# Expert gate marks built as packed 16-bit products with the tokens innermost, and the index products of all heads in one instruction

## The chip, the cores and the metric

The kernel runs on one core of one Trainium2 chip. The metric is the device time of one execution in microseconds (us); the kernel before and the changed kernel are compared by the median of their runs.

## The reference, cut to what matters

The network has four mixer layers, a neighbourhood-attention block and, at the end, a product-key expert layer (`peer_ffn`). The change lies in that last layer alone, for 512 tokens, 8 heads and 128 x 128 experts:

```python
q = (xb @ wq).reshape(PEER_BLOCK, PEER_HEADS, 2, PEER_HALF)
s = jnp.einsum('thpd,hpkd->thpk', q, sub_keys)
s_top, i_top = lax.top_k(s, PEER_TOPK)                      # 16 of 128, per half
cand_s = (s_top[:, :, 0, :, None] + s_top[:, :, 1, None, :])
best_s, best_pos = lax.top_k(cand_s.reshape(...), PEER_TOPK)
experts = jnp.take_along_axis(cand_i, best_pos, axis=-1)
g = jax.nn.softmax(best_s, axis=-1)
act = jax.nn.gelu(einsum('thkd,td->thk', expert_u[experts], xb))
out = einsum('thk,thkd->td', g * act, expert_v[experts])
```

The kernel gathers no expert. It computes the hidden value of every expert for every token and multiplies it by a gate matrix that is zero but for the 128 chosen pairs of a token (8 heads x 16). `expert = first * 128 + second`, so the gate of one token is a 128 x 128 matrix: a product of one-hot rows of `second` (marks B) with one-hot rows of `first` times the gate (marks A).

## The kernel before, in words

Five engines run their own programs: TensorE (PE), VectorE (DVE), ScalarE (ACT), GpSimd (POOL), and SyncE (SP), which issues the weight loads. They meet through semaphores; each engine's order is the order in which its code is written.

**Expert layer, first half (`hidden_units`).** 32 slots of 512 experts pass through two ring buffers. In each slot four chunks `j` are split in two parts (ACT at L1586 makes the first, POOL at L2502 the second; `second_parts`), PE does 16 matmuls of 512 columns for each chunk (L1144, L1145), ACT applies gelu (L1625). Slots 14 to 29 also make the gates: after each chunk's 16 matmuls PE does 16 small ones of 128 columns (`gate_groups`, L1165), B marks stationary, A marks moving, once for the high part of the gate (`l` = 0) and once for its rest (`l` = 1); ACT moves the result to SBUF (L1616) with tokens innermost, and it is stored to DRAM.

**Routing (DVE, `routing`).** While PE runs the first slots, DVE picks the top 16 for four token tiles `t`. L2265 adds candidate scores, one instruction for each head. For each half `s`, L2288 compares positions with a ruler (128 x 2048), L2291 multiplies by the key indices, one instruction of 128 x 256 for each head, and L2295 sums. `r_shifted` (at L2281 of the last tile) lets ACT take the softmax exponent, and ACT does nothing else until then. L2300 is the last step of the choice.

**Turning the choice.** PE finishes slot 12, stops in `turn_choices` until the choice is made (L1139, 12 transposes), then does slot 13. ACT copies the three turned matrices from PSUM (L1649) for DVE.

**Marks (DVE, `gate_marks`).** 32 batches of 16 tokens (`GC`), two buffers. For each token L2316 is one instruction (compare the 128 numbers with `first`, times the two gate parts, 256 results); L2323 makes the B marks of the batch (128 x 2048, 16-bit). PE waits at chunks 0 and 2 of each slot for a batch; DVE waits before batch n until PE has used batch n - 2.

Of the kernel before, what the change touches and what calls it, by code (L numbers as in the profile page):

```python
# [5 lines left out]
P = 128  # L6
D = 1024
S = 512
# [17 lines left out]
PEER_HEADS, N_KEYS = 8, 128  # L26
# [98 lines left out]
def build(nc, wstream, cols_d, const_d, rows_d, pos_d, x_d, ctx_d, rpb_d, ws_d, out_d):  # L125
# [9 lines left out]
    ds = bass.ds  # L135

    with ExitStack() as ctx:
# [310 lines left out]
        R_SUM = area(1856, 16)  # L448
        R_BV = area(6144, NT, 8, 16)
        R_E = area(6656, NT, 3, P)  # L450
        E_T = [trig.rearrange("p a t c -> p (a t c)"), rs[:, 0, :], rs[:, 1, :]]

        U_SLOTS = N_KEYS // 4
        GATE_FROM, GATE_TO = 14, 30
# [6 lines left out]
        G_B = area(28672, 2, GC, N_KEYS // 2).bitcast(f16)  # L461
        G_IOTA = area(30720, N_KEYS // 2).bitcast(f16)
        G_PARTS = area(30784, 2, S)
        G_ROUND = area(31808, S // 2).bitcast(f16)
        G_SECOND = area(32064, S // 2).bitcast(f16)
        GATE_SCALE = 32768.0
        SPREAD = 128.0
        E_CHUNKS = ROWS_S * U_SLOTS
# [106 lines left out]
        def _(pe):  # L575
# [571 lines left out]
            def hidden_units():  # L1147

                made, used, taken = signal("e_parts_made"), signal("e_parts_used"), signal("u_taken")
                first_hot, second_hot = signal("g_a_made"), signal("g_b_made")  # L1150
                gated, kept = signal("g_summed"), signal("g_kept")

                def gate_groups(i, p, j):

                    batch = 2 * (2 * i + p - GATE_FROM) + j // 2
                    if j % 2 == 0:
                        pe.wait_ge(first_hot, batch + 1)
                        pe.wait_ge(second_hot, batch + 1)
                    for x in range(2):
                        g, b = 8 * (2 * i + p - GATE_FROM) + 2 * j + x, 2 * (j % 2) + x  # L1160
                        if not (isinstance(g, int) and g < 4):
                            pe.wait_ge(kept, g - 3)
                        for t in range(4):
                            for l in range(2):
                                mm = pe.matmul(bank[:, 4 + b, t * P:(t + 1) * P], G_B[:, j // 2, 4 * b + t, :],  # L1165
                                               G_A[:, j // 2, 4 * b + t, l, :], start=(l == 0), stop=(l == 1))
                        mm.then_inc(gated, 1)

                def slot(i, p, gates=False):
                    for j in range(4):  # L1170
                        pe.wait_ge(made, 8 * i + 4 * p + j + 1)
                        if not (first(i) and p == 0):
                            pe.wait_ge(taken, 8 * i + 4 * p + j - 3)
                        for k in range(KT):
                            mm = expert_product(bank[:, j, :], j, k, h2_rounded[:, k, :], h2_rest[:, k, :],
                                                k == 0, k == KT - 1)
                        mm.then_inc(used, 1)
                        if gates:
                            gate_groups(i, p, j)

                def both(i, gates=False):
                    slot(i, 0, gates)
# [102 lines left out]
        def _(act):  # L1285
# [318 lines left out]
            def hidden_units():  # L1604
# [134 lines left out]
        def _(dve):  # L1739
# [506 lines left out]
            def routing():  # L2246
# [4 lines left out]
                for t in range(NT):  # L2251
# [7 lines left out]
                    if t == 0:  # L2259
# [1 line left out]
                    sv = R_SV.rearrange("p (h s) j -> p h s j", s=2)  # L2261
                    ins = v.tensor_tensor(R_CAND[:, :, 0:16], sv[:, :, 0, 0:1].broadcast_to([P, 8, 16]),
                                          sv[:, :, 1, :], ALU.add)
                    for h in range(PEER_HEADS):
                        ins = v.tensor_tensor(  # L2265
                            R_CAND[:, h, 16:136].rearrange("p (i j) -> p i j", i=15),
                            sv[:, h, 0, 1:16].rearrange("p (i a) -> p i a", a=1).broadcast_to([P, 15, 8]),
                            sv[:, h, 1, 0:8].rearrange("p (a j) -> p a j", a=1).broadcast_to([P, 15, 8]), ALU.add)
# [17 lines left out]
                    for s in range(2):  # L2286

                        order(v.tensor_tensor(R_EQ, R_RF[:, s, :].rearrange("p (k a) -> p k a", a=1)  # L2288
                                              .broadcast_to([P, P, 16]), iota16, ALU.is_equal))
                        for h in range(PEER_HEADS):  # L2290
                            ins = v.tensor_tensor(R_EQ2[:, h * 16:(h + 1) * 16, :], R_EQ[:, h * 16:(h + 1) * 16, :],  # L2291
                                                  sif[:, h, s, :].rearrange("p (a j) -> p a j", a=1)
                                                  .broadcast_to([P, 16, 16]), ALU.mult)
                        order(ins)
# [12 lines left out]
            def gate_marks():  # L2307
                first_hot, second_hot, gated = signal("g_a_made"), signal("g_b_made"), signal("g_summed")

                def body(m):  # L2310
                    for b in range(2):
                        n = 2 * m + b
                        if not first(m):
                            dve.wait_ge(gated, 4 * n - 4)
                        for t in range(GC):
                            ins = v.scalar_tensor_tensor(  # L2316
                                out=G_A[:, b, t], in0=cst("iota").rearrange("p (l r) -> p l r", l=1)
                                .broadcast_to([P, 2, N_KEYS]), scalar=E_T[0][:, ds(n * GC + t, 1)],
                                in1=G_PARTS[:, :, ds(n * GC + t, 1)].broadcast_to([P, 2, N_KEYS]),
                                op0=ALU.is_equal, op1=ALU.mult)  # L2320
                        ins.then_inc(first_hot, 1)
                        e = G_SECOND[:, ds(n * GC, GC)].rearrange("p (t a) -> p t a", a=1)
                        v.tensor_tensor(G_B[:, b], G_IOTA.rearrange("p (a r) -> p a r", a=1)  # L2323
                                        .broadcast_to([P, GC, N_KEYS]), e.broadcast_to([P, GC, N_KEYS]),
                                        ALU.is_equal).then_inc(second_hot, 1)
                dve.wait_ge(signal("choice_moved"), 3)
                v.tensor_copy(G_IOTA, cst("iota"))
                v.tensor_copy(G_SECOND, E_T[1])
                order(v.tensor_scalar(G_ROUND, E_T[2], GATE_SCALE, None, ALU.mult))
                order(v.tensor_copy(G_PARTS[:, 0, :], G_ROUND))  # L2330
                order(v.scalar_tensor_tensor(out=G_PARTS[:, 1, :], in0=E_T[2], scalar=GATE_SCALE,
                                             in1=G_PARTS[:, 0, :], op0=ALU.mult, op1=ALU.subtract))
                body(0)
                with dve.Fori(1, S // GC // 2) as m:
                    body(m)
# [346 lines left out]
```

## Time and profile before

| | us |
|---|---|
| median of 3 runs (2893.05 to 2898.33) | 2895.91 |
| the profiled execution, its time | 2900.16 |
| its span from first to last instruction | 2898.3 |
| PE busy / DVE busy / POOL busy | 2657.9 / 1856.9 / 1643.7 |
| mean granted TensorE clock, share of full | 0.961 |

The profiled execution is 4.25 us, 0.15%, above the median. Busy shares are means over many stages with different limits; what the change is worth is read from the stretch between 1690 and 2380 us of the span.

### The profile page before, as it was taken

What the parts mean: (1) busy time and instruction counts of PE and PEld (TensorE: products, weight loads), DVE (VectorE), ACT (ScalarE), POOL (GpSimd) and SP (SyncE); (2) the same over time, 40 slices, a digit from 0 to 9 for tenths busy, and PEclk for the clock granted to TensorE, in tenths of its full rate; (3) what the DMA queues carried; (4) which work ended last, traced back from release to release, by engine and by line L of the source; (5) the groups of instructions that cost most, each with busy time, mean ns of one, the idle gap of its engine ahead of it and who ended that gap; (6) DMA issues with size and microseconds to landing.
All of it is one profiled execution on the core that took longest, in us unless ns stands there. A gap on an engine that the chain in (4) does not pass through costs nothing.

```text
span 2898.3 us, 36976 instructions
## 1 busy us (share of the span) xinstructions
PE 2657.9 (92%) x13468; PEld 2140.2 (74%) x13468; DVE 1856.9 (64%) x3298; ACT 949.5 (33%) x1656; POOL 1643.7 (57%) x964
## 2 busy tenths in 40 slices
PE   7999999999899999999899999918777889999998
PEld 6888787678767788788677888816565667888886
DVE  6432398744664444200365079999999966888886
ACT  2001312833474101111242144314343444444443
POOL 4665457965403566646645557616455556666673
PEclk9999999999999999999999999959898999999998
DMA  4223122122342322322213245514454558888883
GB/s 157 87 87 121 58 88 94 31 66 77 110 146 109 116 92 112 109 88 101 98 41 111 92 175 217 217 44 182 170 217 200 217 217 306 290 289 289 289 289 131
DMA packets 139988, 429.93 MB, mean 148 GB/s; under 512 B 8800, under 2 KB 79584, under 8 KB 116704
## 3 DMA queue, kind: packets, MB, share of 16 engines
q1 hardware_dynamic: 125376, 353.40, 33.8%
q10 hardware_dynamic: 7200, 68.68, 6.1%
q0 software_dynamic: 7296, 6.31, 0.9%
q8 instruction: 72, 1.18, 0.2%
q14 instruction: 44, 0.36, 0.0%
HBM read 358.10 MB, written 73.40 MB: 149 GB/s over the span
## 4 chain that ended last, share of the span: by engine, by line
PE 64%; DVE 18%; issue 8%; POOL 6%; DMA 2%; ACT 1%; DVEq 1%; SPq 0%; ACTq 0%; POOLq 0%
PE bank L1144 8%; PE bank L1145 8%; DVE work L2316 6%; PE bank L697 4%; PE bank L698 4%; PE bank L700 4%; POOL rpb_tiles L2464 3%; PE bank L958 3%; PE bank L953 3%; PE bank L954 3%; PE bank L755 3%; PE bank L727 3%; PE bank L749 3%; PE bank L728 3%; PE bank L732 3%
## 5 line engine op out<-in xcount | busy, mean ns | idle before, releaser
L2502 POOL TENSOR_TENSOR expert_parts<-ring,expert_parts 128x1024 fp32r<-128x1024 f32 x256 | 696.3, 2722 | 495.4 <-ACT expert_parts L1586 492.7
L2526 POOL CAST w_parts<-ring 128x1024 fp32r<-128x1024 f32 (+3 forms) x212 | 228.8, 1079 | 636.3 <-DMA ring<-in_wstream 153.0
L2528 POOL TENSOR_TENSOR w_parts<-ring,w_parts 128x1024 fp32r<-128x1024 f32 (+3 forms) x212 | 512.1, 2416 | 17.0
L1586 ACT ACTIVATE expert_parts<-ring 128x1024 fp32r<-128x1024 f32 x256 | 271.2, 1060 | 538.5 <-PE bank L1145 531.0
L1144 PE MATMUL bank<-h_rounded,expert_parts 128*128 128x512 f32 x1024 | 414.0, 404 | 0.7 <-ACT work L1598 0.7
L1144 PE MATMUL bank<-weighted,expert_parts 128*128 128x512 f32 x1024 | 401.9, 393 | 9.9 <-DVE weighted L2348 9.9
L1145 PE MATMUL bank<-h_rest,expert_parts 128*128 128x512 f32 x1024 | 406.1, 397 | 0.0
L1145 PE MATMUL bank<-weighted,expert_parts 128*128 128x512 f32 x1024 | 401.5, 392 | 0.0
L2316 DVE SCALAR_TENSOR_TENSOR work<-const,trig,work 128x256 f16<-128x256 f32 x512 | 346.3, 748 | 0.0
L2348 DVE SCALAR_TENSOR_TENSOR weighted<-weighted,hF 128x512 fp32r<-128x512 f32 x128 | 309.5, 2419 | 51.3 <-ACT weighted L1666 48.1
L1144 PEld LDWEIGHTS bank<-weighted,expert_parts 128*128 128x128 f32 x1024 | 194.2, 190 | 51.2 <-issue 6.0
L1144 PEld LDWEIGHTS bank<-h_rounded,expert_parts 128*128 128x128 f32 x1024 | 197.9, 193 | 41.5 <-ACT work L1598 0.9
L1145 PEld LDWEIGHTS bank<-h_rest,expert_parts 128*128 128x128 f32 x1024 | 197.5, 193 | 40.1
L1145 PEld LDWEIGHTS bank<-weighted,expert_parts 128*128 128x128 f32 x1024 | 194.3, 190 | 40.7
L697 PE MATMUL bank<-h_parts,w_parts 128*128 128x512 f32 x480 | 186.9, 389 | 0.5 <-POOL w_parts L2528 0.5
L698 PE MATMUL bank<-h_parts,w_parts 128*128 128x512 f32 x480 | 186.8, 389 | 0.0
L1165 PE MATMUL bank<-work 128*128 128x128 f16 x1024 | 74.8, 231 | 89.4 <-DVE work L2323 80.6
L1165 PEld LDWEIGHTS bank<-work 128*128 128x128 f16 x1024 | 63.2, 104 | 109.7 <-issue 109.7
L2353 DVE TENSOR_TENSOR hF<-hF,work 128x512 f32<-128x512 f32 x128 | 97.8, 783 | 46.6 <-DMA work<-gates 46.6
L1518 ACT ACTIVATE work<-bank 128x512 f32<-128x512 f32 (+1 forms) x58 | 32.6, 586 | 264.4 <-PE bank L958 180.7
L700 PE MATMUL bank<-h_parts,w_parts 128*128 128x512 f32 x480 | 118.5, 389 | 0.0
L749 PE MATMUL bank<-w_parts,b_rounded 128*128 128x512 f32 (+3 forms) x320 | 116.9, 372 | 0.7 <-ACT work L1421 0.7
(430 smaller groups left out, 5155.4 us busy)
## 6 DMA issues: line engine op xcount, KB each, us to landing
ring<-in_wstream SPq DMA_DIRECT2D x128, 2048.0 KB, 7.8
hidden<-hF ACTq DMA_DIRECT2D x32, 1024.0 KB, 4.0
gates<-work ACTq DMA_DIRECT2D x16, 2048.0 KB, 10.7
hF<-hidden SPq DMA_DIRECT2D x32, 1024.0 KB, 9.5
work<-gates SPq DMA_DIRECT2D x32, 1024.0 KB, 12.8
rpb_tiles<-in_rpb POOLq DMA_DIRECT2D x192, 16.0 KB, 2.2
work<-rpb_tiles POOLq DMA_DIRECT2D x24, 128.0 KB, 5.4
ring<-in_wstream SPq DMA_DIRECT2D x5, 512.0 KB, 4.0
```

The lines of the kernel that those rows point to most:

```text
L697: pe.matmul(out, w[0][:, k, :], h_parts[:, 0, k, :], start=(k == 0), stop=False)
L698: pe.matmul(out, w[1][:, k, :], h_parts[:, 0, k, :], start=False, stop=False)
L700: mm = pe.matmul(out, w[0][:, k, :], h_parts[:, 1, k, :], start=False, stop=(k == KT - 1))
L749: pe.matmul(out, x, w[0][:, k - ks[0], :], start=(k == 0), stop=False)
L1144: pe.matmul(out, expert_chunk(j, 0)[:, k, :], x, start=start, stop=False)
L1145: return pe.matmul(out, expert_chunk(j, 1)[:, k, :], x_spread, start=False, stop=stop)
L1586: act.activation(expert_chunk(j, 0), ring_chunk(p, j), ACT.Copy, scale=1.0 - 1.0 / SPREAD)\
L2316: ins = v.scalar_tensor_tensor(out=G_A[:, b, t], in0=cst("iota").rearrange("p (l r) -> p l r", l=1) .broadcast_to([P, 2, N_KEYS]), scalar= ...
L2348: v.scalar_tensor_tensor(out=W[:, 4 * p + j, 1, :], in0=W[:, 4 * p + j, 0, :], scalar=1.0 - SPREAD, in1=hF[:, 4 * p + j, :], op0=ALU.mult, ...
L2502: nc.gpsimd.tensor_tensor(expert_chunk(j, 1), ring_chunk(p, j), expert_chunk(j, 0), ALU.subtract).then_inc(made, 1)
L2526: g.tensor_copy(parts[0], source).then_inc(hi, 1)
L2528: g.tensor_tensor(parts[1], source, parts[0], ALU.subtract).then_inc(made, 1)
```

## The change

Four edits. (1) A marks: instead of 16 instructions with 32-bit inputs, a batch takes three 16-bit products of 128 x 2048 with the 16 tokens innermost: a comparison of a ruler with `first`, that times the high part, that times the rest. The moving operand of the small matmuls so becomes one 16-bit number in every 16 (a step of 32 bytes). (2) B marks are made by the same instruction as before, now between the comparison and the products. (3) ACT's three copies go; DVE reads the turned choice from PSUM itself, and writes the ruler before it. (4) In `routing` the eight instructions of L2265 and the eight of L2291 become one each.

```diff
-        G_A = area(24576, 2, GC, N_KEYS).bitcast(f16).rearrange("p b t (l r) -> p b t l r", l=2)
+        G_A = area(24576, 2, 2 * N_KEYS * GC // 2).bitcast(f16).rearrange("p b (l r t) -> p b l r t", l=2, t=GC)
+        G_RULER = area(30720, N_KEYS * GC // 2).bitcast(f16).rearrange("p (r t) -> p r t", t=GC)
+        G_HIGH, G_LOW = (area(31744 + j * S // 2, S // 2).bitcast(f16) for j in range(2))
...
                                 mm = pe.matmul(bank[:, 4 + b, t * P:(t + 1) * P], G_B[:, j // 2, 4 * b + t, :],
-                                               G_A[:, j // 2, 4 * b + t, l, :], start=(l == 0), stop=(l == 1))
+                                               G_A[:, j // 2, l, :, 4 * b + t], start=(l == 0), stop=(l == 1))
...
-                pe.wait_ge(signal("choice_moved"), 3)
...
-                for c in range(3):
-                    act.wait_ge(signal("choice_turned"), c + 1)
-                    act.activation(E_T[c], bank[:, 4 + c, :], ACT.Copy).then_inc(signal("choice_moved"), 1)
...
-                    for h in range(PEER_HEADS):
-                        ins = v.tensor_tensor(
-                            R_CAND[:, h, 16:136].rearrange("p (i j) -> p i j", i=15),
+                    ins = v.tensor_tensor(
+                        R_CAND[:, :, 16:136].rearrange("p h (i j) -> p h i j", i=15),
...
-                        for h in range(PEER_HEADS):
-                            ins = v.tensor_tensor(R_EQ2[:, h * 16:(h + 1) * 16, :], R_EQ[:, h * 16:(h + 1) * 16, :],
+                        order(v.tensor_tensor(R_EQ2.rearrange("p (h k) j -> p h k j", h=PEER_HEADS),
...
-                        for t in range(GC):
-                            ins = v.scalar_tensor_tensor(
...
-                                op0=ALU.is_equal, op1=ALU.mult)
-                        ins.then_inc(first_hot, 1)
...
+                        order(v.tensor_tensor(G_A[:, b, 1], G_RULER, of(G_FIRST, n), ALU.is_equal))
+                        v.tensor_tensor(G_B[:, b], G_ROW.rearrange("p (a r) -> p a r", a=1).broadcast_to([P, GC, N_KEYS]),
...
+                        order(v.tensor_tensor(G_A[:, b, 0], G_A[:, b, 1], of(G_HIGH, n), ALU.mult))
+                        v.tensor_tensor(G_A[:, b, 1], G_A[:, b, 1], of(G_LOW, n), ALU.mult).then_inc(first_hot, 1)
+                order(v.tensor_copy(G_RULER, cst("iota").rearrange("p (r a) -> p r a", a=1).broadcast_to([P, N_KEYS, GC])))
+                dve.wait_ge(signal("choice_turned"), 3)
...
+                order.laps(S // GC // 2, body, 4)
```

`of(x, n)` is the batch's 16 tokens of `x`, repeated for the 128 numbers: its innermost step is one 16-bit number. `order(...)` waits until the instruction has ended; `order.laps` writes the loop over pairs of batches.

On DVE, the end of the last token tile's routing reads before as follows (`work` is the big SBUF area, `rs` holds the top scores and indices, `const` the ruler):

```order
-L2281 TENSOR_TENSOR work<-work 128x128
-L2288 TENSOR_TENSOR work<-work,const 128x2048
-L2291 TENSOR_TENSOR work<-work,rs 128x256 x8
-L2295 TENSOR_REDUCE work<-work 128x128
-L2288 TENSOR_TENSOR work<-work,const 128x2048
-L2291 TENSOR_TENSOR work<-work,rs 128x256 x8
-L2295 TENSOR_REDUCE work<-work 128x128
```

and now:

```order
+L2276 TENSOR_TENSOR work<-work 128x128
+L2283 TENSOR_TENSOR work<-work,const 128x2048
+L2285 TENSOR_TENSOR work<-work,rs 128x2048
+L2289 TENSOR_REDUCE work<-work 128x128
+L2283 TENSOR_TENSOR work<-work,const 128x2048
+L2285 TENSOR_TENSOR work<-work,rs 128x2048
+L2289 TENSOR_REDUCE work<-work 128x128
```

The order stays; eight products of 256 have become one of 2048, and the lines have moved up.

Behind the choice, DVE's preparation and first two batches read before (`trig` and `rs` hold the turned choice):

```order
-L2327 CAST work<-const 128x128
-L2328 CAST work<-rs 128x512
-L2329 TENSOR_SCALAR work<-rs 128x512
-L2330 CAST work<-work 128x512
-L2331 SCALAR_TENSOR_TENSOR work<-rs,work 128x512
-L2316 SCALAR_TENSOR_TENSOR work<-const,trig,work 128x256 x16
-L2323 TENSOR_TENSOR work<-work 128x2048
-L2316 SCALAR_TENSOR_TENSOR work<-const,trig,work 128x256 x16
-L2323 TENSOR_TENSOR work<-work 128x2048
```

and now (`bank` is PSUM):

```order
+L2318 CAST work<-const 128x2048
+L2320 CAST work<-const 128x128
+L2321 CAST rs<-bank 128x512
+L2322 CAST rs<-bank 128x512
+L2323 TENSOR_SCALAR work<-bank 128x512
+L2324 SCALAR_TENSOR_TENSOR work<-bank,work 128x512
+L2312 TENSOR_TENSOR work<-work,rs 128x2048
+L2313 TENSOR_TENSOR work<-work,rs 128x2048
+L2316 TENSOR_TENSOR work<-work 128x2048
+L2317 TENSOR_TENSOR work<-work 128x2048
```

A batch is four instructions where it was seventeen; the B marks (L2323 before, L2313 now) are second where they were last. On PE the order is the same in both kernels.

## Rows read from the trace of the kernel before

**Rows 1.** Stretches: length, busy us (count) of PE, PEld, DVE, ACT, POOL; clock; DMA

```profile
1750.00:1800.00 50.00, 50.00 (x222) 41.39 (x221) 49.31 (x221) 21.34 (x28) 33.99 (x15) 1.00 0.52 200
1886.00:1948.00 62.00, 0.00 (x0) 0.00 (x0) 60.83 (x242) 7.75 (x10) 10.03 (x4) 0.52 0.13 51
1955.00:2370.00 415.00, 325.63 (x2072) 263.56 (x2071) 413.49 (x543) 167.62 (x260) 215.15 (x67) 0.91 0.50 197
```

**Rows 2.** Waits from 1880 to 1975 us: who waited for whom, us, times, longest

```profile
PE bank L1139 <- DVE work L2300: 62.8, 1, 62.8
ACT work L1645 <- DVE work L2281: 47.0, 1, 47.0
```

**Rows 3.** Waits from 1955 to 2380 us

```profile
PE bank L1165 <- DVE work L2323: 80.6, 21, 7.6
```

**Rows 4.** PE's transposes and small matmuls: ns min/median/max, first and last start

```profile
L1139 PE MATMUL bank<-const,work x12: 421/421/474, 1948.5 to 1950.9; 128*128 128x128 f32 x12
...
L1165 PE MATMUL bank<-work x1024: 217/219/314, 1970.6 to 2374.2; 128*128 128x128 f16 x171
```

**Rows 5.** DVE's groups by line and form: busy us, mean ns | idle before

```profile
L2316 DVE SCALAR_TENSOR_TENSOR work<-const,trig,work 128x256 f16<-128x256 f32 x512 | 346.3, 748 | 0.0
...
L2291 DVE TENSOR_TENSOR work<-work,rs 128x256 f32<-128x256 f32 x64 | 63.1, 1054 | 0.3
...
L2288 DVE TENSOR_TENSOR work<-work,const 128x2048 f32<-128x2048 f32 x8 | 19.2, 2399 | 0.1
...
L2265 DVE TENSOR_TENSOR work<-rs 128x120 f32<-128x120 f32 x32 | 15.3, 547 | 0.0
```

**Rows 6.** The marks' line alone: ns min/median/max, first and last start

```profile
L2316 DVE SCALAR_TENSOR_TENSOR work<-const,trig,work x512: 468/473/2657, 1954.2 to 2365.8; 128x256 f16<-128x256 f32 x171
```

**Rows 7.** DVE's timeline at the last tile: start us, us, engine, line

```profile
1907.76 1.63 DVE L2265 TENSOR_TENSOR work<-rs 128x120 f32<-128x120 f32 x8
...
1921.63 2.28 DVE L2288 TENSOR_TENSOR work<-work,const 128x2048 f32<-128x2048 f32 x1
1923.95 11.23 DVE L2291 TENSOR_TENSOR work<-work,rs 128x256 f32<-128x256 f32 x8
1935.22 2.29 DVE L2295 TENSOR_REDUCE work<-work 128x128 f32<-128x2048 f32 x1
...
1939.86 2.77 DVE L2291 TENSOR_TENSOR work<-work,rs 128x256 f32<-128x256 f32 x8
```

**Rows 8.** POOL's timeline there

```profile
1923.40 10.16 POOL L2502 TENSOR_TENSOR expert_parts<-ring,expert_parts 128x1024 fp32r<-128x1024 f32 x4 [47.66 <-ACT expert_parts L1586]
```

**Rows 9.** DVE's timeline, two batches of marks

```profile
2018.20 2.28 DVE L2323 TENSOR_TENSOR work<-work 128x2048 f16<-128x2048 f16 x1
2020.40 14.91 DVE L2316 SCALAR_TENSOR_TENSOR work<-const,trig,work 128x256 f16<-128x256 f32 x16
...
2037.43 6.02 DVE L2316 SCALAR_TENSOR_TENSOR work<-const,trig,work 128x256 f16<-128x256 f32 x15
```

**Rows 10.** PE's timeline, one chunk with its small matmuls, and a burst at the lower clock

```profile
2062.17 0.47 PE L1144 MATMUL bank<-h_rounded,expert_parts 128*128 128x512 f32 x1
...
2065.91 1.07 PE L1165 MATMUL bank<-work 128*128 128x128 f16 x16
2066.79 0.47 PE L1144 MATMUL bank<-h_rounded,expert_parts 128*128 128x512 f32 x1
...
2089.01 1.89 PE L1165 MATMUL bank<-work 128*128 128x128 f16 x16 [7.62 <-DVE work L2323]
```

**Rows 11.** ACT's reads of PSUM, strided (L1616) and packed (L1625)

```profile
L1616 ACT ACTIVATE work<-bank x128: 586/596/601, 1972.3 to 2375.5; 128x512 f32<-128x512 f32 x128
...
L1625 ACT ACTIVATE hF<-bank x128: 575/578/605, 1706.7 to 2404.5; 128x512 f32<-128x512 f32 x128
```

**Rows 12.** DVE with one input and with two, 512 elements each

```profile
L2329 DVE TENSOR_SCALAR work<-rs x1: 418/418/418, 1952.5 to 1952.5; 128x512 f16<-128x512 f32 x1
...
L1770 DVE TENSOR_TENSOR h_parts<-hF,h_parts x16: 681/684/687, 28.2 to 966.3; 128x512 fp32r<-128x512 f32 x16
```

More of the change, by code:

```diff
@@ L450, in build @@
         R_E = area(6656, NT, 3, P)
-        E_T = [trig.rearrange("p a t c -> p (a t c)"), rs[:, 0, :], rs[:, 1, :]]
         U_SLOTS = N_KEYS // 4
@@ L459, in build @@
         G_STAGE = area(0, 2, N_KEYS, GT)
-        G_A = area(24576, 2, GC, N_KEYS).bitcast(f16).rearrange("p b t (l r) -> p b t l r", l=2)
[L461 to L465, printed above, removed]
+        G_A = area(24576, 2, 2 * N_KEYS * GC // 2).bitcast(f16).rearrange("p b (l r t) -> p b l r t", l=2, t=GC)
+        G_B = area(28672, 2, N_KEYS * GC // 2).bitcast(f16).rearrange("p b (t r) -> p b t r", t=GC)
+        G_ROW = area(32256, N_KEYS // 2).bitcast(f16)
+        G_RULER = area(30720, N_KEYS * GC // 2).bitcast(f16).rearrange("p (r t) -> p r t", t=GC)
+        G_HIGH, G_LOW = (area(31744 + j * S // 2, S // 2).bitcast(f16) for j in range(2))
+        G_FIRST, G_SECOND = (rs[:, j, 0:S // 2].bitcast(f16) for j in range(2))
         GATE_SCALE = 32768.0
@@ L2263, in routing @@
                                           sv[:, :, 1, :], ALU.add)
-                    for h in range(PEER_HEADS):
-                        ins = v.tensor_tensor(
-                            R_CAND[:, h, 16:136].rearrange("p (i j) -> p i j", i=15),
-                            sv[:, h, 0, 1:16].rearrange("p (i a) -> p i a", a=1).broadcast_to([P, 15, 8]),
-                            sv[:, h, 1, 0:8].rearrange("p (a j) -> p a j", a=1).broadcast_to([P, 15, 8]), ALU.add)
+                    ins = v.tensor_tensor(
+                        R_CAND[:, :, 16:136].rearrange("p h (i j) -> p h i j", i=15),
+                        sv[:, :, 0, 1:16].rearrange("p h (i a) -> p h i a", a=1).broadcast_to([P, PEER_HEADS, 15, 8]),
+                        sv[:, :, 1, 0:8].rearrange("p h (a j) -> p h a j", a=1).broadcast_to([P, PEER_HEADS, 15, 8]),
+                        ALU.add)
                     order(ins)
@@ L2289, in routing @@
                                               .broadcast_to([P, P, 16]), iota16, ALU.is_equal))
-                        for h in range(PEER_HEADS):
-                            ins = v.tensor_tensor(R_EQ2[:, h * 16:(h + 1) * 16, :], R_EQ[:, h * 16:(h + 1) * 16, :],
-                                                  sif[:, h, s, :].rearrange("p (a j) -> p a j", a=1)
-                                                  .broadcast_to([P, 16, 16]), ALU.mult)
-                        order(ins)
+                        order(v.tensor_tensor(R_EQ2.rearrange("p (h k) j -> p h k j", h=PEER_HEADS),
+                                              R_EQ.rearrange("p (h k) j -> p h k j", h=PEER_HEADS),
+                                              sif[:, :, s, :].rearrange("p h (a j) -> p h a j", a=1)
+                                              .broadcast_to([P, PEER_HEADS, 16, 16]), ALU.mult))
                         order(v.reduce_sum(R_E[:, t, s, :], R_EQ2, AX))
@@ L2310, in body, with of @@
                 def body(m):
+                    def of(x, n):
+                        return x[:, ds(n * GC, GC)].rearrange("p (a t) -> p a t", a=1).broadcast_to([P, N_KEYS, GC])
                     for b in range(2):
@@ L2314, in body @@
                             dve.wait_ge(gated, 4 * n - 4)
-                        for t in range(GC):
-                            ins = v.scalar_tensor_tensor(
-                                out=G_A[:, b, t], in0=cst("iota").rearrange("p (l r) -> p l r", l=1)
-                                .broadcast_to([P, 2, N_KEYS]), scalar=E_T[0][:, ds(n * GC + t, 1)],
-                                in1=G_PARTS[:, :, ds(n * GC + t, 1)].broadcast_to([P, 2, N_KEYS]),
-                                op0=ALU.is_equal, op1=ALU.mult)
@@ L2321, in body @@
-                        ins.then_inc(first_hot, 1)
[L2322 to L2335, printed above, removed]
+                        order(v.tensor_tensor(G_A[:, b, 1], G_RULER, of(G_FIRST, n), ALU.is_equal))
@@ new lines, in body @@
+                        v.tensor_tensor(G_B[:, b], G_ROW.rearrange("p (a r) -> p a r", a=1).broadcast_to([P, GC, N_KEYS]),
+                                        G_SECOND[:, ds(n * GC, GC)].rearrange("p (t a) -> p t a", a=1)
+                                        .broadcast_to([P, GC, N_KEYS]), ALU.is_equal).then_inc(second_hot, 1)
+                        order(v.tensor_tensor(G_A[:, b, 0], G_A[:, b, 1], of(G_HIGH, n), ALU.mult))
+                        v.tensor_tensor(G_A[:, b, 1], G_A[:, b, 1], of(G_LOW, n), ALU.mult).then_inc(first_hot, 1)
@@ new lines, in gate_marks @@
+                order(v.tensor_copy(G_RULER, cst("iota").rearrange("p (r a) -> p r a", a=1).broadcast_to([P, N_KEYS, GC])))
+                dve.wait_ge(signal("choice_turned"), 3)
+                v.tensor_copy(G_ROW, cst("iota"))
+                v.tensor_copy(G_FIRST, bank[:, 4, :])
+                v.tensor_copy(G_SECOND, bank[:, 5, :])
+                order(v.tensor_scalar(G_HIGH, bank[:, 6, :], GATE_SCALE, None, ALU.mult))
+                order(v.scalar_tensor_tensor(out=G_LOW, in0=bank[:, 6, :], scalar=GATE_SCALE, in1=G_HIGH,
+                                             op0=ALU.mult, op1=ALU.subtract))
```

## The prediction, made before the changed kernel was run

> **What bounds the kernel now.** I read the stretches first, then the waits, then the groups of DVE, then the timelines. The reader should see two places in the expert layer where PE, which is otherwise full there (50.00 of 50 us, [rows 1]), waits for DVE.
>
> The first is the choice. From 1886 to 1948 PE does nothing while DVE is busy 60.8 of 62 us [rows 1]: its transposes wait 62.8 us for L2300, once [rows 2]. PE stopped at 1948.5 - 62.8 = 1885.7. ACT stood still for the same reason, 47.0 us, until L2281 [rows 2].
>
> The second is the gate stretch: first small matmul at 1970.6, last at 2374.2 [rows 4]. DVE is busy 413.5 of 415 us, PE 325.6 at a mean granted clock of 0.91 [rows 1]; PE's waits for marks sum to 80.6 us [rows 3]. From the choice (1948.5) to the last small matmul it is 425.7 us, of which the first 22.1 are the transposes and slot 13.
>
> Beneath both lies a third thing: DVE is held by POOL. L2316 takes 473 ns in the median, 748 in the mean, 2657 at most [rows 5, 6]. The 512 instructions so lose 512 x 0.275 = 141 us; POOL did 67 instructions there [rows 1], so each of them held DVE for about 2.1 us. In routing, eight L2291 take 2.77 us free and 11.23 us beside four POOL instructions [rows 7, 8]: 2.1 us a hold. POOL's instruction waits until DVE's has ended, DVE's next one waits until POOL's has ended. L2323 and L2295 are not stretched where they stand [rows 7, 9].
>
> Check of the bound: a batch without holds is 16 x 0.396 us (15 in 6.02, the last 0.47, [rows 9]) + 2.2 = 8.54; 32 x 8.54 + 141 = 414 us, DVE's busy time there. So DVE sets the pace.
>
> **The choice.** L2291 takes 63.1 us [rows 5], free it would be 8 x 2.77 = 22.2; 40.9 us are some 19 holds. L2265 takes 15.3 [rows 5], free 4 x 1.63 [rows 7] = 6.5; four holds. One product of 128 x 2048 with two 32-bit inputs costs what L2288 costs, 2.28 [rows 7] to 2.40 with its own holds [rows 5]; I take 2.3. The merged L2265 has 960 elements; from 684 ns for 512 [rows 12] and 2.28 for 2048 it is 1.15 us.
>
> How many holds stay? POOL has an instruction each 50 / 15 = 3.3 us while PE runs [rows 1]. One that comes during L2288 (2.3 us) gets its turn before the merged product, so about 0.65 x 2.1 = 1.4 us for each of the six pairs beside running slots. Those six took 63.1 - 11.2 - 2.8 = 49.1; they become 6 x 3.7 = 22.2: 27 saved. The four merged sums take 4 x 1.15 + 1.6 for less than one hold = 6.2: 9 saved. So `r_shifted` moves from 1921.6 to 1885.6, just where PE stops; ACT is then released at once and POOL's four instructions come as before, against the last tile. There the pair of L2291 took 14.0; it becomes 2 x 2.3 + two holds = 8.9, since POOL runs beside the reductions: 5 saved. The choice falls at 1948.5 - 41 = **1907.5**, and PE waits 22 us instead of 62.8. Bounds: no hold at all saves 55 us, a hold before each merged instruction 30.
>
> **The preparation** costs nothing on the path. The ruler's copy (at most 2.3 us, as a 2048-element instruction) lies beside PE's transposes (1948.5 to 1950.9, [rows 4]); the reads of PSUM are four of 0.7 us where ACT's copies and DVE's casts stood before the first batch, which started 5.7 us after the choice (1954.2, [rows 6]). Slot 13 covers all of it: PE asks for marks only 22.1 us after the choice. Without that cover it would be 6 us, once. ACT's copies leave an engine that is not the bound.
>
> **The marks.** A batch is now three products at a price `a`, and the B marks, unchanged, at 2.28 [rows 9]. No row has a two-input 16-bit instruction with all patterns packed. One bound is one result per cycle, 2.28. The other is the pace of packed one-input work: 418 ns against 684 for 512 elements [rows 12], 0.52 ns per element less, so 2.28 - 2048 x 0.00052 = 1.21. L2323 has 16-bit operands too but one of them stands still along the innermost dimension; the new three have none that does. I take 1.21. A batch is 3 x 1.21 + 2.28 + 0.1 for the waits on its own results = 6.0, plus two holds (64 POOL instructions in 32 batches) 4.3 = 10.3 us. DVE alone would end the stretch at 5.7 + 32 x 10.3 + 6 (PE's last chunks) = 341 us after the choice.
>
> The Trainium skill, "VectorE: DVE Perf Modes", section on the perf-mode tier table, says that tensor_tensor with 16-bit SBUF operands of step 1 gives two results per cycle, 1224 ns for 2048. By that figure a batch would be 6.05 + holds, the same sum; no run here shows it yet.
>
> **The moving operand.** PE reads A marks in steps of 32 bytes now. The packed pitch is (1.07 - 0.22) / 15 = 57 ns, a chunk with its 16 small matmuls 2066.79 - 2062.17 = 4.62 us [rows 4, 10]. No row has a strided moving operand. One bound is no loss, 57 ns. The other is the nearest strided read: ACT takes 596 ns for 512 numbers 512 bytes apart [rows 11], at most 1.16 ns each, 149 ns for 128. Between them is the array's own lower pace: a burst at a granted clock of half took (1.89 - 0.31) / 15 = 105 ns [rows 10]. I take 105, a column at 0.8 ns, because ACT's row shows a fresh place in memory at about that pace and nothing faster. A chunk becomes 4.62 + 16 x 0.048 = 5.39, a slot 21.6, and PE's end 22.1 - 3.6 + 16 x 21.6 = 364 us after the choice. PE, not DVE, then sets the pace, by 1 us a slot; 3 us more for batches that holds make late: 367.
>
> The Trainium skill, "Advanced Engine Details and Errata", section on memory cachelines, speaks against the change here: lines of 16 bytes, two hits on a line needed for full pace, a penalty otherwise. Each column here is alone on its line. It gives no figure; ACT's strided row is only 18 ns slower than its packed one, which does not show the loss it also claims for PSUM.
>
> **Sum**, against the profiled time 2900.2: choice -41, gate stretch 367 - 425.7 = -58.7, behind it nothing (slots 30, 31 and the second half start earlier, unchanged): 2800.5. The profiled time is 0.15% above the median; by that share **2797 us**.
>
> **Rivals.**
> (a) *The stride costs nothing.* DVE sets the end: 341 + 3 = 344, so -41 - 81.7: 2777 in the profile's time, 2773 by median. For it: ACT's row. Against it: nothing here reads at PE's 57 ns with a step.
> (b) *The products run at one per cycle.* A batch is 4 x 2.28 + 0.1 + 4.3 = 13.5, the end 5.7 + 32 x 13.5 + 6 = 444: the marks lose 18 us, the choice keeps 41: 2877, or 2873. For it: the one 16-bit row, 2.28. Against it: that row's operand stands still.
> (c) *Slower: the moving read costs so much that PE's small matmuls become the bound.* The choice's 41 us are eaten when the stretch reaches 466.7, a slot 28.0, a chunk 7.0, a small matmul 57 + 149 = 206 ns. At four times the packed pitch, 228 ns, a chunk is 7.36, the stretch 489: +64 - 41 = 2923, or 2918. For it: every column on a fresh line. Against it: ACT's 1.16 ns per number would be 149 ns.
> (d) *The choice gains little*, because POOL's instructions, no longer spent on L2291, hold other routing work: 30 saved instead of 41, 2811, or 2807.
>
> **How the numbers follow.** 0.2% (5.8 us) is about what a measurement of this kernel can tell from no change. Chances: forecast 0.45, (a) 0.33, (b) 0.12, (c) 0.06, (d) 0.04. The range starts at (a) with every hold gone from routing (14 us more, 2760) and ends at the forecast with the stride at its bound of 149 ns (a chunk 6.09, the stretch 411, 2841); it leaves out (b) and (c), 0.18. The forecast's own range is 2785 to 2815. Faster 0.92, same 0.02, slower 0.06.
>
> **What would show each step.** PE's wait before the transposes near 22 us. The merged product near 2.3 us, sometimes 4.4. The three products near 1.2 us, the B marks still 2.28. PE's burst of 16 small matmuls: 1.07 us if the stride is free, about 1.8 at my price, over 3.3 if (c). In the gate stretch PE near full and DVE with some idle time before a batch, waiting for PE; under (a) DVE full and PE waiting on the marks. I am wrong above all if the burst stays at 1.07 or the products stay at 2.28.

## The result, and the profile after

| | us |
|---|---|
| before, median of 4 runs (2893.05 to 2898.33) | 2895.07 |
| changed, median of 4 runs (2962.9 to 2968.07) | 2965.2 |
| ratio, with its 95% interval | 1.0242 (1.0224 to 1.0259) |
| the changed kernel's profiled execution, its time / span | 2968.07 / 2966.3 |
| its PE / DVE / POOL busy | 2836.1 / 1663.1 / 1606.8 |

The changed kernel is 2.4% slower; 2797 was forecast. DVE has 194 us less work, and PE is busy 178 us longer.

The gate stretch first, with the columns of [rows 1], and two pieces of it, 2.7 us behind one burst of small matmuls and 3.7 us behind the next:

```profile
1950.00:2450.00 500.00, 500.00 (x2042) 328.99 (x2041) 220.15 (x121) 174.11 (x255) 150.38 (x64) 0.94 0.42 163
...
2052.70:2055.40 2.70, 2.70 (x9) 2.12 (x8) 2.10 (x2) 0.60 (x1) 0.13 (x1) 0.62 0.06 24
...
2061.70:2065.40 3.70, 3.70 (x18) 2.94 (x16) 0.00 (x0) 0.60 (x1) 0.12 (x1) 1.00 0.00 0
```

The roles have changed: PE has no idle time in 500 us, DVE is busy for 220 of them. The waits from 1880 to 2460 us say the same; where PE waited for marks [rows 3], DVE now waits for PE:

```profile
DVE work L2312 <- PE bank L1164: 243.7, 30, 10.2
...
PE bank L1138 <- DVE work L2294: 40.7, 1, 40.7
ACT work L1643 <- DVE work L2276: 28.3, 1, 28.3
```

The other two rows are the choice [rows 2]: PE waits 40.7 us for it, not 62.8, and ACT 28.3, not 47.0.

PE's timeline from 2049 us, one chunk with the bursts of small matmuls (now L1164) at its ends, against [rows 10]:

```profile
2049.14 3.87 PE L1164 MATMUL bank<-work 128*128 128x128 f16 x16
...
2052.65 0.60 PE L1143 MATMUL bank<-h_rounded,expert_parts 128*128 128x512 f32 x1
...
2054.56 0.63 PE L1144 MATMUL bank<-h_rest,expert_parts 128*128 128x512 f32 x1
...
2058.13 3.87 PE L1164 MATMUL bank<-work 128*128 128x128 f16 x16
```

A burst takes 3.87 us where it took 1.07. Less the last matmul's 0.41, that is 3.46 / 15 = 231 ns for a small matmul of 128 columns (232 from the second one on), 57 before. From burst to burst it is 8.99 us here and 7.36 in most other places.

The changed instructions, each line by itself (ns min/median/max, first and last start), against [rows 4 to 6]:

```profile
L1164 PE MATMUL bank<-work x1024: 390/412/412, 1947.0 to 2444.8; 128*128 128x128 f16 x171
...
L1138 PE MATMUL bank<-const,work x12: 417/417/472, 1924.8 to 1927.2; 128*128 128x128 f32 x12
...
L2285 DVE TENSOR_TENSOR work<-work,rs x8: 4310/4373/4384, 1733.9 to 1914.6; 128x2048 f32<-128x2048 f32 x8
...
L2283 DVE TENSOR_TENSOR work<-work,const x8: 2282/4424/4484, 1729.4 to 1910.2; 128x2048 f32<-128x2048 f32 x8
...
L2259 DVE TENSOR_TENSOR work<-rs x4: 1150/1154/3343, 1711.7 to 1887.9; 128x960 f32<-128x960 f32 x4
...
L2318 DVE CAST work<-const x1: 1217/1217/1217, 1924.7 to 1924.7; 128x2048 f16<-128x2048 f32 x1
...
L2312 DVE TENSOR_TENSOR work<-work,rs x32: 1224/1225/3420, 1930.5 to 2414.3; 128x2048 f16<-128x2048 f16 x32
...
L2313 DVE TENSOR_TENSOR work<-work,rs x32: 2291/2291/4369, 1931.8 to 2415.7; 128x2048 f16<-128x2048 f16 x32
...
L2316 DVE TENSOR_TENSOR work<-work x32: 1215/1218/3418, 1934.0 to 2417.9; 128x2048 f16<-128x2048 f16 x32
```

The choice falls at 1924.8 us of the span, where the first transpose starts, 23.7 earlier. The stretch from there to the last small matmul is 2444.8 - 1924.8 = 520.0 us, 94.3 more than before. 94.3 - 23.7 = 70.6; the span grew by 68.0, so 2.6 us come back elsewhere.

**What the 520 us are.** 22.2 us to the first burst; 63 distances from burst to burst; 3.5 us of the last burst. 44 of the distances are 7.36 us and 19 are some 8.98, 494.4 together. In the long ones the granted clock falls to half (1.2 GHz) for a few us of the 512-column matmuls behind a burst, though the profile shows no idle time of PE before: 0.62 in the mean from 2052.7 to 2055.4 above, and 1.00 behind the next burst, from 2061.7 to 2065.4. The 19 falls cost 19 x 1.62 = 31 us.

### The profile page after: what moved, and what is told of

Its sections match the earlier page's. It is cut to its first block, busy times and chain, and to the rows that moved or that the text cites. A ratio compares the mean times of both kernels' runs of the same rounds, so it can differ in the third digit from the quotient of the medians.

```text
span 2966.3 us, 36145 instructions
## 1 busy us (share of the span) xinstructions
PE 2836.1 (96%) x13468; PEld 2208.3 (74%) x13468; DVE 1663.1 (56%) x2799; ACT 958.3 (32%) x1653; POOL 1606.8 (54%) x964
## 4 chain that ended last, share of the span: by engine, by line
PE 80%; DVE 10%; POOL 5%; DMA 2%; ACT 1%; issue 1%; SPq 0%; ACTq 0%; DVEq 0%; POOLq 0%
PE bank L1143 13%; PE bank L1144 13%; PE bank L1164 8%; PE bank L696 4%; PE bank L697 4%; PE bank L699 4%; POOL rpb_tiles L2455 3%; PE bank L957 3%; PE bank L952 3%; PE bank L953 3%; PE bank L726 3%; PE bank L727 3%; PE bank L731 3%; PE bank L754 3%; PE bank L748 2%; PE bank L749 2%
## 5 line engine op out<-in xcount | busy, mean ns | idle before, releaser
L2493 POOL TENSOR_TENSOR expert_parts<-ring,expert_parts 128x1024 fp32r<-128x1024 f32 x256 | 656.3, 2567 | 606.8 <-ACT expert_parts L1584 605.7
L1143 PE MATMUL bank<-h_rounded,expert_parts 128*128 128x512 f32 x1024 | 431.7, 422 | 0.7 <-ACT work L1596 0.7
L1144 PE MATMUL bank<-h_rest,expert_parts 128*128 128x512 f32 x1024 | 417.8, 408 | 0.0
L1164 PE MATMUL bank<-work 128*128 128x128 f16 x1024 | 247.8, 410 | 0.0
L1143 PEld LDWEIGHTS bank<-h_rounded,expert_parts 128*128 128x128 f32 x1024 | 205.1, 200 | 51.1 <-ACT work L1596 0.9
L1144 PEld LDWEIGHTS bank<-h_rest,expert_parts 128*128 128x128 f32 x1024 | 204.9, 200 | 43.8
L1164 PEld LDWEIGHTS bank<-work 128*128 128x128 f16 x1024 | 112.7, 115 | 118.7 <-issue 16.9
L2312 DVE TENSOR_TENSOR work<-work,rs 128x2048 f16<-128x2048 f16 x32 | 41.4, 1294 | 243.8 <-PE bank L1164 243.7
```

The source lines that it names most:

```text
L1143: pe.matmul(out, expert_chunk(j, 0)[:, k, :], x, start=start, stop=False)
L1144: return pe.matmul(out, expert_chunk(j, 1)[:, k, :], x_spread, start=False, stop=stop)
L2493: nc.gpsimd.tensor_tensor(expert_chunk(j, 1), ring_chunk(p, j), expert_chunk(j, 0), ALU.subtract).then_inc(made, 1)
```

## The experiments

Eleven kernels. Where several executions were timed, the ratio is to the kernel before, run again beside them on the same chip: its medians were 2905.94 us (packed read, routing alone), 2898.64 (groups of two and of four) and 2897.54 (marks alone, both in pairs, 16-bit routing).

### Is it the stride alone?

The changed kernel with one edit: PE reads the same number of A marks as if they lay packed (`G_FLAT` is the buffer of the A marks without its layout).

```diff
-                                               G_A[:, j // 2, l, :, 4 * b + t], start=(l == 0), stop=(l == 1))
+                                               G_FLAT[:, j // 2, (2 * (4 * b + t) + l) * P:(2 * (4 * b + t) + l + 1) * P], start=(l == 0), stop=(l == 1))
```

> Everything of the change stays, but the small matmuls read their moving operand packed (128 neighbouring 16-bit numbers of the same buffer), so the gates are not the reference's. Theory 1, the step of 32 bytes is the whole loss: the burst of 16 small matmuls falls from 3.87 to 1.07 us, DVE sets the pace with 10.4 us a batch, the stretch from the choice to the last small matmul is about 345 us where it is 520 now, and the time is 2965 - 175 = about 2790. Rival, the reads are slow because DVE writes the same area or because of the way the marks are made: the burst stays above 3 us and the time near 2965. The short dips of the granted clock in that stretch go under theory 1 and stay under the rival.

Measured: 2785.08 us (2781.22 to 2790.59), ratio 0.9582 (0.9539 to 0.9624). The small matmuls' line, and PE's waits from 1880 to 2290 us:

```profile
L1165 PE MATMUL bank<-work x1024: 219/219/230, 1944.4 to 2259.8; 128*128 128x128 f16 x171
```

```profile
PE bank L1139 <- DVE work L2295: 38.2, 1, 38.2
...
PE bank L1165 <- DVE work L2318: 18.3, 29, 0.8
```

The bursts are back at 56 ns, the stretch of small matmuls is 315 us and not 498, and PE waits for marks again, a little. The granted clock of the stretch is 1.00, without a fall. So the stride, with the falls that come with it, is the whole loss: the ratio falls from 1.0242 to 0.9582, and the rest of the change is worth 4%.

### What does PE pay for?

The same read with another step in each of a slot's four chunks; in the second kernel the first chunk reads two neighbouring numbers every 32 bytes.

```diff
-                                               G_A[:, j // 2, l, :, 4 * b + t], start=(l == 0), stop=(l == 1))
+                                               moved(j, 2 * t + l), start=(l == 0), stop=(l == 1))
...
+                    k, flat = (1, 2, 4, 8)[j], G_FLAT[:, j // 2, :]
...
+                    return flat[:, 0:P * k].rearrange("p (r c) -> p r c", c=k)[:, :, at % k]
```

> As the changed kernel, but chunk 0 of each gated slot reads its moving operand in steps of 2 bytes, chunk 1 of 4, chunk 2 of 8, chunk 3 of 16, all within the same buffers (the gates are not the reference's). If the pace is set by lines of 16 bytes, with two numbers of a line enough, the small matmul takes 57, 57, 57 and 232 ns. If the price grows with the bytes passed over (232 ns at 32 bytes), it takes 57, 57, 58 and 116 ns. If any step but the packed one is slow, 57, 232, 232, 232.

> As the changed kernel, but chunk 0 reads pairs of neighbours every 32 bytes, chunk 1 single numbers every 24 bytes, chunk 2 every 32, chunk 3 every 64 (the gates are not the reference's). Lines of 16 bytes: the pairs 57 to 116 ns, the rest 232 each. Bytes passed over: pairs 116, then 174, 232 and 464 ns. Any step but the packed one: 232 for all singles, pairs the same.

Measured: 2845.67 and 2910.27 us, one execution each. Bursts in PE's timeline, small steps (in this order 4, 8, 16 and 2 bytes):

```profile
2049.80 1.10 PE L1171 MATMUL bank<-work 128*128 128x128 f16 x16
...
2054.45 2.02 PE L1171 MATMUL bank<-work 128*128 128x128 f16 x16
...
2059.94 3.79 PE L1171 MATMUL bank<-work 128*128 128x128 f16 x16
...
2067.23 1.07 PE L1171 MATMUL bank<-work 128*128 128x128 f16 x16
```

and large steps (64 bytes, the pairs, 24 and 32 bytes):

```profile
2055.70 3.63 PE L1171 MATMUL bank<-work 128*128 128x128 f16 x16
...
2062.85 2.04 PE L1171 MATMUL bank<-work 128*128 128x128 f16 x16
...
2068.39 3.79 PE L1171 MATMUL bank<-work 128*128 128x128 f16 x16
...
2075.66 3.87 PE L1171 MATMUL bank<-work 128*128 128x128 f16 x16
```

From start to start within a burst, 128 columns take 56, 58, 116 and 227 ns at steps of 2, 4, 8 and 16 bytes, then 227, 232 and 217 at 24, 32 and 64; the pairs take 118. So from 4 bytes on the price doubles with the step until each column has 16 bytes of its own, and changes little from there. It is about 1.8 ns for each 16 bytes touched (232 / 128 = 1.81; 116 / 64 lines = 1.81; 118 / 64 = 1.84; 217 / 128 = 1.70), or 0.44 ns for each column where that is more (56 / 128).

For the small steps none of the three expectations came as it was written: with lines of 16 bytes and two numbers enough 57 ns was expected at 8 bytes, and it is 116; with a price by bytes passed over 58 and 116 were expected at 8 and 16 bytes, and they are 116 and 227; and a step of 4 bytes, at 58, is not slow. The large steps decide for lines: singles 24 and 64 bytes apart cost nearly the same (227 and 217), where bytes passed over would have given 174 and 464.

The Trainium skill, "Advanced Engine Details and Errata", section on memory cachelines, has the 16-byte lines and the penalty right, and asks for two hits on a line. Here two 16-bit numbers on a line cost twice the packed time (116 against 56 ns); four cost 2 ns.

### The two halves of the change

Before with the merged routing alone, and the changed kernel with the routing of before:

```diff
-                    for h in range(PEER_HEADS):
-                        ins = v.tensor_tensor(
...
+                    ins = v.tensor_tensor(
...
-                        for h in range(PEER_HEADS):
-                            ins = v.tensor_tensor(R_EQ2[:, h * 16:(h + 1) * 16, :], R_EQ[:, h * 16:(h + 1) * 16, :],
...
+                        order(v.tensor_tensor(R_EQ2.rearrange("p (h k) j -> p h k j", h=PEER_HEADS),
```

> The kernel before with the merged index products and candidate sums alone. If the trace of the changed kernel tells the price of that part (the choice came 24 us earlier), 2895 - 24 = 2871, each of the eight merged products about 4.4 us and each comparison ahead of it about 4.4 while POOL works. Rival, the part is worth the 41 us of the prediction and the changed kernel lost 17 of them to its other edits: 2854.

> The changed kernel with the routing of before: the sums and the index products are again one instruction for each head, the marks and PE's strided reading stay as changed. Nothing is left out. Theory one, the two parts add: the choice falls where it did before, 24 us later than in the changed kernel, and all of it is PE's; 2965 + 24 = 2989 us, some 1.032 of before. Rival, the merged products only moved DVE's waiting: 1.024, as the changed kernel.

Measured: routing alone 2876.94 us, ratio 0.9897 (0.9854 to 0.9939); marks alone 2994.81, ratio 1.0325 (1.0293 to 1.0357). Of routing alone, the product's line, and PE's wait:

```profile
L2290 DVE TENSOR_TENSOR work<-work,rs x8: 4311/4378/4389, 1736.1 to 1916.6; 128x2048 f32<-128x2048 f32 x8
```

```profile
PE bank L1139 <- DVE work L2299: 38.1, 1, 38.1
```

The halves add up: 0.9897 x 1.0325 = 1.0219, and by the intervals of the two factors it is uncertain by about 0.005, which takes in the 1.0242 measured. The merged routing gains 1% by itself: PE's wait is 24.7 us shorter, and the profiled execution 22.6 (2877.54 against 2900.16), so nearly all of it reaches the end. With the marks alone PE waits 62.8 us for the choice, as before. One expectation failed in part: with the routing alone the comparisons were held in four of eight (3.34 us in the mean), not in each.

### Who holds the merged products?

The packed read, with POOL's instruction cut to an eighth after the first pair of slots:

```diff
-                            nc.gpsimd.tensor_tensor(expert_chunk(j, 1), ring_chunk(p, j), expert_chunk(j, 0),
...
+                            nc.gpsimd.tensor_tensor(expert_chunk(j, 1)[:, 0:n, :], ring_chunk(p, j)[:, 0:n, :],
+                                                    expert_chunk(j, 0)[:, 0:n, :], ALU.subtract).then_inc(made, 1)
...
+                pair(0, 8)
+                with pool.Fori(1, U_SLOTS) as i:
+                    pair(i, 1)
```

> The packed read once more (A marks read as if they lay packed, so gates are not the reference's), and POOL makes its second parts in full only for the first pair of slots, later only an eighth of each, so that its instruction is about an eighth as long (the rest of the second parts is then stale and the experts' hidden values are not the reference's). Theory one, DVE is held by POOL for as long as POOL's instruction lasts: the merged products of the routing go back to 2.3 us and the comparisons to 2.28, PE's wait for the choice falls from 38 us to below 10, a batch takes 6.2 us and PE waits for no marks; about 2785 - 35 - 18 = 2730 us. Rival, the merged products take 4.3 us for another reason (their own shape): PE's wait for the choice stays above 30 us, and the time above 2755.

Measured: 2728.84 us, one execution. DVE's groups (busy us, mean ns), and the waits:

```profile
L2286 DVE TENSOR_TENSOR work<-work,rs 128x2048 f32<-128x2048 f32 x8 | 19.5, 2433 | 0.3
L2284 DVE TENSOR_TENSOR work<-work,const 128x2048 f32<-128x2048 f32 x8 | 18.3, 2288 | 0.1
```

```profile
DVE work L2313 <- PE bank L1165: 94.5, 30, 8.5
...
PE bank L1139 <- DVE work L2295: 4.5, 1, 4.5
```

The merged product takes 2.43 us, the comparison 2.29, PE waits 4.5 us for the choice and for no marks. Theory one holds: what the choice lacks is POOL's holds.

### The same marks with a smaller step

The A marks in groups of `TB` tokens, 2 or 4 in place of 16: tokens of a group innermost, then the 128 numbers, then the groups.

```diff
-        G_A = area(24576, 2, 2 * N_KEYS * GC // 2).bitcast(f16).rearrange("p b (l r t) -> p b l r t", l=2, t=GC)
...
+        G_A = area(24576, 2, 2 * N_KEYS * GC // 2).bitcast(f16).rearrange("p b (l g r t) -> p b l g r t", l=2, r=N_KEYS, t=TB)
...
-                                               G_A[:, j // 2, l, :, 4 * b + t], start=(l == 0), stop=(l == 1))
+                                               G_A[:, j // 2, l, (4 * b + t) // TB, :, (4 * b + t) % TB], start=(l == 0), stop=(l == 1))
...
```

> The changed kernel with the A marks laid out in pairs of tokens: two tokens innermost, then the 128 numbers, then the pairs. PE's moving operand then has a step of 4 bytes, and the three products keep 16-bit operands with no one standing still along the innermost dimension, but an inner run of 2 numbers. Nothing is left out. Theory one, PE pays for every 16-byte line that it does not use with at least four numbers: small matmuls at 58 ns, no clock dips of note, and a time like the packed read's, 0.958 of before. Within it two ways for DVE: the products keep two results per cycle (1.22 us, three of them and B marks 2.29 and two holds, 10.3 us a batch; 0.955 to 0.965), or the short inner run throws them back to one per cycle (2.29 us, 13.5 us a batch, DVE the bound, about 2875 us, 0.99). Rival, any step at all costs PE the 232 ns of the changed kernel when the marks are the true ones: 1.02.

> The same with groups of 4 tokens, a step of 8 bytes: two numbers on a 16-byte line. Nothing is left out. Theory one: small matmuls at 116 ns, a chunk 4.62 + 16 x 0.06 = 5.58 us, a slot 22.3, 3.86 us more for each of 16 slots than packed; PE, not DVE, is then close to the bound, some 20 to 50 us behind groups of two: 0.965 to 0.98, with some clock dips. Rival, two numbers on a line are enough: like groups of two.

Measured: pairs 2785.47 us (2780.57 to 2804.26), ratio 0.9614 (0.9583 to 0.9644); groups of four 2821.06, ratio 0.9724 (0.9694 to 0.9753). Of the pairs, a product with 16-bit operands and the B marks:

```profile
L2314 DVE TENSOR_TENSOR work<-work,rs x32: 1210/1212/3422, 1941.4 to 2257.1; 128x2048 f16<-128x2048 f16 x32
...
L2316 DVE TENSOR_TENSOR work<-work,rs x32: 2293/4270/4386, 1942.7 to 2258.5; 128x2048 f16<-128x2048 f16 x32
```

DVE keeps two numbers per cycle with an inner run of two, and PE's small matmul takes 58 ns: pairs have all of DVE's gain without PE's price, and within the intervals give the packed read's ratio (0.9582) with nothing left out. With groups of four (116 ns) PE is the bound again, every chunk 5.49 us long; the clock's dips that were expected did not come (1.00 over the stretch). DVE waits for PE:

```profile
DVE work L2314 <- PE bank L1165: 35.2, 30, 1.2
```

### Does the stationary operand pay as well, and can it be used?

The packed read, with the stationary operand read in steps of 2, 4, 8 and 32 bytes in the four chunks; then, with nothing left out, the A and the B marks both in pairs; then that with a 16-bit comparison result, 16-bit key indices and 16-bit product in the routing.

```diff
-                                mm = pe.matmul(bank[:, 4 + b, t * P:(t + 1) * P], G_B[:, j // 2, 4 * b + t, :],
+                                mm = pe.matmul(bank[:, 4 + b, t * P:(t + 1) * P], held(j, 4 * b + t),
...
-        G_B = area(28672, 2, N_KEYS * GC // 2).bitcast(f16).rearrange("p b (t r) -> p b t r", t=GC)
+        G_B = area(28672, 2, N_KEYS * GC // 2).bitcast(f16).rearrange("p b (g r t) -> p b g r t", r=N_KEYS, t=TB)
...
-        R_EQ = area(2048, P, 16)
-        R_EQ2 = area(4096, P, 16)
+        R_EQ = area(2048, P, 8).bitcast(f16)
+        R_EQ2 = area(4096, P, 8).bitcast(f16)
```

> Moving operand packed as in the packed read, and the stationary operand (B marks) read in steps of 2, 4, 8 and 32 bytes for the chunks 0, 1, 2 and 3 of each slot (gates are not the reference's). Theory one, the price per line is the same for a weight load, and the loads are as many as the small matmuls: bursts at 56, 58, 116 and 230 ns. Rival, the price is the moving read's alone: 56 ns in all four, and the time within 0.3% of the packed read's 2785.

> A and B marks both laid out in pairs of tokens, so that all four products of a batch have 16-bit operands without one that stands still along the innermost dimension; PE's stationary operand then has a step of 4 bytes too (56 ns as packed, by the run on the stationary steps). Nothing is left out. Theory one: B marks fall from 2.29 to 1.22 us, a batch to 4 x 1.22 + 0.5 + 4.3 = 9.7 us at most, PE's slot stays at 18.5 us for two batches; PE and DVE are level, the gate stretch is about 15 us shorter than with groups of two, the ratio to before 0.953 to 0.960. Rival: with shorter instructions POOL gets its turns more often, DVE's batch stays at 10 us by holds, and the time is that of groups of two, 0.961.

> The same, and in the routing the comparison's result, the key indices and the merged product are 16-bit (all of them are whole numbers up to 127). Nothing is left out. Theory one: the merged product takes 1.22 us and one hold, 3.3 where it took 4.36, so 8 x 1.06 = 8 us less ahead of the choice, the comparison as before; PE's wait for the choice falls from 40.7 to some 32 us, the ratio is 0.003 below that of both in pairs. Rival: one hold for each instruction whatever its length, and POOL paced by its count: no gain beyond 2 us.

Measured: 2800.74 us (one execution); 2766.11 (2761.83 to 2769.3), ratio 0.9538 (0.9512 to 0.9563); 2752.1 (2742.6 to 2768.78), ratio 0.9507 (0.9479 to 0.9535). Bursts of the first, a step of 8 bytes and then of 32, and their line by itself:

```profile
2050.76 1.08 PE L1170 MATMUL bank<-work 128*128 128x128 f16 x16 [0.64 <-DVE work L2323]
...
2055.40 1.22 PE L1170 MATMUL bank<-work 128*128 128x128 f16 x16
```

```profile
L1170 PE MATMUL bank<-work x1024: 219/219/278, 1961.4 to 2277.0; 128*128 128x128 f16 x171
```

The stationary operand pays hardly anything: 56 ns up to 8 bytes, about 62 at 32. The time, 15.7 us above the packed read's, is outside the 0.3% that the rival gave, but its small matmuls take 315.6 us from first to last and the packed read's 315.4; they start 17 us later. The difference lies ahead of the stretch, and most of it ahead of the choice: PE stops for the choice at 1899.0 us here and at 1884.2 there, in code that is the same in both.

So B marks may lie in pairs too. The stretch of that kernel, and the B marks:

```profile
1950.00:2243.00 293.00, 293.00 (x2024) 240.41 (x2022) 264.35 (x122) 159.03 (x253) 206.65 (x63) 1.00 0.70 277
```

```profile
L2316 DVE TENSOR_TENSOR work<-work,rs x32: 1225/3201/3303, 1934.8 to 2226.2; 128x2048 f16<-128x2048 f16 x32
```

PE is full at the full clock (1.00), a chunk is 4.65 us, and the small matmuls take 293.6 us from first to last where groups of two took 316.0. The B marks take 1.23 us free, but 3.20 in the median: 31 of the 32 are still held. In the last kernel the product and PE's wait are:

```profile
L2287 DVE TENSOR_TENSOR work<-work,rs x8: 3243/3304/3312, 1726.6 to 1894.7; 128x2048 f16<-128x2048 f16 x8
```

```profile
PE bank L1140 <- DVE work L2296: 27.1, 1, 27.1
```

The product takes 3.30 us as expected. The comparison, expected as before (4.16 in the mean), also fell, to 3.36, since four of the eight were not held, and the wait is 27.1, not 32. Only the profile tells this kernel's time from the one without the 16-bit routing: their intervals overlap. Both beat the changed kernel, and are 4.6 and 4.9% below the kernel before.

## Why the prediction was wrong

The step that failed is **The moving operand**. It took 105 ns for a small matmul and, as its upper bound, 149 ns, "the nearest strided read", ACT's; the runs show 232. That bound was none: ACT's row is another engine that reads another memory (PSUM), so it bounds nothing on PE's read of SBUF. Nor was the 596 ns the price of a fresh place in memory: ACT's packed read of as many numbers takes 578 ns [rows 11], so the row shows little but ACT's own pace. With that row the prediction also set aside the warning that it names, of 16-byte lines with each column alone on its own. The middle value, the pace at half clock, was no property of the read either. Two resources of the change had no row of their own, the strided read and the 16-bit products; for the products the bounds came from DVE itself and held.

By the sum's own terms, all in profiled time: 63 x (7.36 - 5.39) = 124 us for the stride, 31 for the clock's falls behind the bursts, 2 for the longer last burst, less 3 for late batches that did not come, and 17 for the choice are 171; 2.6 come back elsewhere. The profiled execution is 2968.1 - 2800.5 = 168 above the forecast.

Rival (c) was the case. Its place, chunk (7.36 us), sign (a burst over 3.3 us) and direction are what was measured. That its 228 ns came so near 232 is luck: no row stood behind "four times the packed pitch". It fell 47 us short by the median (2918 against 2965): the clock's falls, which no part foresaw, and the choice's smaller gain (31 + 17). Its chance, 0.06, hung on ACT's row alone.

**The choice** was mis-sized: 41 us forecast, 24 measured, 6 below the lower bound. Its prices were right (2.43 and 2.29 us without holds, 1.15 for the sum), and the count of holds was not. I counted POOL's turns by its instructions in the time that the free work takes; but a held instruction lasts 4.4 us, longer than POOL's 3.6 us from one start to the next there, so that POOL's next one is ready when it ends. L2285 was held in all eight, and the comparisons, hardly held before (2.40 us in the mean, [rows 5]), in seven of eight:

```profile
L2285 DVE TENSOR_TENSOR work<-work,rs 128x2048 f32<-128x2048 f32 x8 | 34.9, 4361 | 0.3
...
L2283 DVE TENSOR_TENSOR work<-work,const 128x2048 f32<-128x2048 f32 x8 | 33.3, 4162 | 0.1
```

The comparisons' 33.3 us where they took 19.2 are 14 of the 17 us; the products, 34.9 where the prediction had 31.1, are the rest. The sum put nothing for new holds on the comparison. Shorter DVE work in fewer pieces moved holds on to its neighbours, as rival (d) said of other routing work.

**The marks** were right: 1.22 us forecast as 1.21, B marks 2.29. The Trainium skill's figure in "VectorE: DVE Perf Modes", the perf-mode tier table, 1224 ns, agrees with the 1224 ns of L2312. Rival (b) is out. With the packed read the stretch from the choice (1922.4) to the last small matmul is 337 us, where rival (a) had 344.

**The preparation** was right: the ruler's copy takes 1.22 us beside the transposes, and PE's first small matmul comes 22.2 us after the choice, as before (22.1).

Rival (a), a free stride, gave 2777 in the profile's time; the packed read, which is that case, took 2783.84 in its profiled execution. Its choice falls at 1922.4, 15 us later than forecast, and its stretch is 7 us shorter than (a) had it; that makes 8 us, where the times differ by 7.

## What to carry to other kernels

A layout that suits VectorE can cost TensorE more than it saves: price the moving operand by the 16-byte lines that it touches, about 1.8 ns each here, against 0.44 ns a column, and give each line at least four 16-bit numbers. A group as small as two tokens already gave VectorE its full pace. And a bound must come from the same engine and the same memory; a row of another engine, however near in kind, left the true price outside the range.

## What was not expected of the hardware

- TensorE's price is on the moving operand nearly alone. The stationary one at a 32-byte step took a matmul from 56 to about 62 ns, the moving one from 56 to 232.
- The granted clock falls to half behind bursts of strided matmuls though the profile shows no idle time of PE: 19 times in the changed kernel (0.94 over its stretch). With steps of 8 bytes throughout it stayed at 1.00; with the small steps mixed it fell 12 times (0.95), with the large ones mixed once (1.00). What sets it off is open, since three of those last kernel's four chunks were as slow as the changed kernel's.
- Two-input VectorE instructions of 2.3 us beside a steady POOL are mostly held once each: the merged product in eight of eight (4.31 to 4.38 us), the comparison ahead of it in seven of eight, but in four of eight in the packed read and with the routing alone. The hold goes with POOL's instruction when that is shortened (2.43 and 2.29).
